# Sixteen zeroing DMAs moved to another stage, and the first use of gathered expert rows moved by eight tiles

## What is computed

```python
def peer_ffn(x, wq, subkeys, u_tab, v_tab):
    q = (xf @ wq).astype(f32).reshape(n, PEER_HEADS, 2, PEER_HALF)
    s = jnp.einsum('nhpd,hpkd->nhpk', q, subkeys.astype(f32))
    top_s, top_i = lax.top_k(s, PEER_TOPK)
    ...
    expert = jnp.take_along_axis(cand_i, best_j, axis=-1)
    gate = jax.nn.softmax(best_s, axis=-1)
    ...
    def one_block(args):
        xb, eb, gb = args
        h = jax.nn.gelu(jnp.einsum('nd,nhkd->nhk', xb, u_tab[eb], preferred_element_type=f32), approximate=False)
        return jnp.einsum('nhk,nhkd->nd', (gb * h).astype(xb.dtype), v_tab[eb])
```

## Time and profile before

| | us |
|---|---|
| median of 3 runs (3161.84 to 3166.44) | 3165.94 |
| the profiled execution | 3163.14 |
| its span | 3161.5 |
| TensorE busy | 2820.4 (89%) |
| VectorE busy | 1805.1 (57%) |
| ScalarE busy | 986.4 (31%) |
| GpSimd busy | 772.3 (24%) |

### The profile page before, as it was taken

One profiled execution on the slowest core, in us unless ns is written; L12 is line 12 of the kernel. 1 busy time (PEld: TensorE's weight loads), 2 busy tenths in 40 slices (PEclk: granted clock), 3 DMA queues, 4 the chain that ended last, 5 costly groups with the idle time before them and its releaser, 6 DMA issues.

```text
span 3161.5 us, 45193 instructions
## 1 busy us (share of the span) xinstructions
PE 2820.4 (89%) x17548; PEld 2427.2 (77%) x17548; DVE 1805.1 (57%) x2598; ACT 986.4 (31%) x1169; POOL 772.3 (24%) x630
## 2 busy tenths in 40 slices
PE   3999984767988999759699997999999999999997
PEld 2999972456666666549599997999999888888886
DVE  3455541198774443233468895555656667666655
ACT  1454530011221111122323233333334434434343
POOL 0100002210000222200018787888840000000000
PEclk7999997687889999879899998999999999999999
DMA  3355434322223555242356666999888888876664
GB/s 124 134 185 182 160 142 126 95 68 63 62 67 107 162 154 155 77 145 105 124 166 173 177 180 173 295 300 289 296 309 304 327 303 306 308 275 249 246 237 176
DMA packets 245312, 594.93 MB, mean 188 GB/s; under 512 B 76345, under 2 KB 180162, under 8 KB 192658
## 3 DMA queue, kind: packets, MB, share of 16 engines
q1 hardware_dynamic: 173874, 484.95, 44.8%
q0 software_dynamic: 54592, 90.41, 10.7%
q10 hardware_dynamic: 16640, 16.78, 1.6%
HBM read 535.05 MB, written 56.97 MB: 187 GB/s over the span
## 4 chain that ended last, share of the span: by engine, by line
PE 31%; POOL 12%; issue 5%; DMA 3%; DVE 1%; ACT 0%; DVEq 0%; POOLq 0%
POOL expert_gates L2122 12%; PE px_bank L272 10%; PE px_bank L274 10%; PE px_bank L273 10%; PE px_bank L2178 1%; DMA expert_gates<-px_chosen,px_spot 1%; POOL px_fetch L2142 1%; DMA px_w<-in_peer_v 1%; DMA px_parts<-sample_parts 0%; DMA px_fetch<-in_peer_rows,px_spots_s 0%; ACT px_wh L2253 0%; DMA px_w<-in_peer_wq 0%; DVE px_rows L2514 0%; DMA px_w<-in_peer_u 0%; DVE px_fetch L2519 0%
## 5 line engine op out<-in xcount | busy, mean ns | idle before, releaser
L2327 DVE TENSOR_TENSOR px_w_r<-px_w,px_wh 128x2048 fp32r<-128x2048 f32 x256 | 585.8, 2291 | 278.9 <-ACT px_wh L2253 278.5
L2253 ACT ACTIVATE px_wh<-px_w 128x2048 fp32r<-128x2048 f32 x256 | 489.8, 1913 | 593.1 <-PE px_bank L274 242.3
L272 PE MATMUL px_bank<-px_high,px_wh 128*128 128x256 f32 x2048 | 584.5, 285 | 24.2 <-DVE px_w_r L2327 24.2
L2122 POOL DMA_INDIRECT expert_gates<-px_chosen,px_spot x256 | 499.0, 1949 | 430.3 <-DVE px_chosen L2401 322.9
L273 PE MATMUL px_bank<-px_low,px_wh 128*128 128x256 f32 x2048 | 581.4, 284 | 0.0
L274 PE MATMUL px_bank<-px_high,px_w_r 128*128 128x256 f32 x2048 | 581.4, 284 | 0.0
L272 PEld LDWEIGHTS px_bank<-px_high,px_wh 128*128 128x128 f32 x2048 | 395.2, 193 | 25.6 <-DVE px_w_r L2327 25.6
L272 PE MATMUL px_bank<-px_wh,px_gh 128*128 128x512 f32 x1024 | 398.5, 389 | 1.2 <-DVE px_gl L2333 1.2
L274 PE MATMUL px_bank<-px_wh,px_gl 128*128 128x512 f32 x1024 | 398.4, 389 | 0.0
L273 PE MATMUL px_bank<-px_w_r,px_gh 128*128 128x512 f32 x1024 | 398.4, 389 | 0.0
L273 PEld LDWEIGHTS px_bank<-px_low,px_wh 128*128 128x128 f32 x2048 | 395.2, 193 | 0.0
(11 more groups left out here) (392 smaller groups left out, 4352.1 us busy)
## 6 DMA issues: line engine op xcount, KB each, us to landing
px_w<-in_peer_u SPq DMA_DIRECT2D x128, 1024.0 KB, 5.4
px_w<-in_peer_v SPq DMA_DIRECT2D x128, 1024.0 KB, 4.9
pj_w<-in_w_in SPq DMA_DIRECT2D x49, 1024.0 KB, 4.9
expert_gates<-rh_empty ACTq DMA_DIRECT2D x16, 1024.0 KB, 6.4
at_values<-in_kv_pages POOLq DMA_DIRECT2D x128, 128.0 KB, 2.7
at_pages<-in_kv_pages SPq DMA_DIRECT2D x128, 128.0 KB, 2.2
out_w<-in_w_o SPq DMA_DIRECT2D x16, 1024.0 KB, 4.8
px_w<-in_peer_wq SPq DMA_DIRECT2D x16, 1024.0 KB, 4.9
```

The source lines that it names most:

```text
L272: pe.matmul(out, w_high, high, start=start, stop=False, skip_group_check=True)
L2122: pool.indirect_dma_start(gates_d, bass.IndirectOffsetOnAxis(ap=spot[:, t, z:z + 1], axis=0), chosen[:, 2, t, z:z + 1], None, compute_op=A ...
L2253: act.activation(w_high[u % WH][:], w[s][:], ACT.Copy).then_inc(raised, 1)
L2327: v.tensor_tensor(w_low[s][:], w[s][:], w_high[u % WH][:], ALU.subtract).then_inc(lowered, 1)
```

## The change

The sixteen zeroing DMAs go from the joint stage to the input projection: ScalarE issues one behind the emptying of chunks 0, 3, 6 to 45, from a tile `nothing` that GpSimd clears first of all; SyncE waits for them at the end of that phase. The old tile, its clearing on VectorE and ScalarE's wait for the DMAs at the end of the joint stage go. In the expert stage the first turn with a gathered tile is u = 50 instead of u = 42; all later turns of the samples follow, so four of the 32 additions move from the up half to the down half.

```diff
@@ in_projection @@
+        nothing = sb("nothing", [P, NP])
+        gates_to = gates_d.rearrange("(z p x n) o -> z p x (n o)", z=16, p=P, n=NP)
@@ sync @@
                 sp.wait_ge(stored, 48)
+                sp.wait_ge(gates_zeroed, 16 * 16)
@@ scalar @@
                     empty(c)
+                    if c % 3 == 0 and c // 3 < 16:
+                        act.wait_ge(nothing_set, 1)
+                        act.dma_start(gates_to[c // 3], nothing[:].rearrange("p (o n) -> p o n", o=1)
+                                      .to_broadcast([P, D // NP, NP])).then_inc(gates_zeroed, 16)
@@ gpsimd @@
+                pool.memset(nothing[:], 0.0).then_inc(nothing_set, 1)
@@ mixers @@
-        empty = sb("empty", [P, NP])
@@ scalar @@
                     done(act.activation(wu_out(0), wu_in(0), ACT.Copy, scale=-1.0), i, "wu")
-                    act.wait_ge(emptied, 1)
-                    for z in (2 * i, 2 * i + 1):
-                        act.dma_start(gates_to[z], empty[:].rearrange("p (o n) -> p o n", o=1)
-                                      .to_broadcast([P, D // NP, NP])).then_inc(cleared, 16)
...
-                act.wait_ge(cleared, 32 * PAIRS)
@@ vector @@
-                v.memset(empty[:], 0.0).then_inc(emptied, 1)
@@ peer_layer @@
     def sample_turn(u):

         if u < NK:
-            return u >= 42 and u % 2 == 0
+            return u >= 50 and u % 2 == 0
         return u % 3 == 1
```

More of the change, by code:

```diff
@@ L373, in build @@
                 cx.phase(split, "x_in", xT, before_mix, x_low)
-                cx.phase(in_projection, a, o, projT, ends, before_mix, x_low, ident, feat_d, post_d, rows_d)
+                cx.phase(in_projection, a, o, projT, ends, before_mix, x_low, ident, feat_d, post_d, rows_d, gates_d)
             bias_rows, vnew_d, mask_d = (scratch(*x) for x in (
@@ L383, in build @@
             cx.phase(mixers, a, o, projT, mixT, ident, ends, feat_d, post_d, rows_d,
-                     (bias_rows, vnew_d, mask_d, wrow, ws, vrows, qi, qb, near, table), gates_d)
+                     (bias_rows, vnew_d, mask_d, wrow, ws, vrows, qi, qb, near, table))
         with ExitStack() as late:
@@ L396, in build, with in_projection @@
         peer(cx, a, o, mixT[:, :, META:N], mixT, ident, gates_d)
-def in_projection(cx, a, o, projT, ends, high, low, ident, feat_d, post_d, rows_d):
+def in_projection(cx, a, o, projT, ends, high, low, ident, feat_d, post_d, rows_d, gates_d):
     nc = cx.nc
@@ L431, in in_projection @@
                  "up_done", "gated", "keyed", "exped", "producted", "normed", "rooted", "featured", "turned", "rowed",
-                 "stored_features", "stored_rows", "link", "stored")
+                 "stored_features", "stored_rows", "link", "stored", "nothing_set", "gates_zeroed")
         (constants, raised, lowered, summed, emptied, cleared, differed, mixed, squashed, up_done, gated, keyed, exped,
          producted, normed, rooted, featured, turned, rowed, stored_features, stored_rows, link,
-         stored) = (cx.sem(f"pj_{x}") for x in names)
+         stored, nothing_set, gates_zeroed) = (cx.sem(f"pj_{x}") for x in names)
         groups = [[C_WA, C_WA + 1, C_WA + 2]] + [[j, 8 + j, 16 + j] for j in range(PAIRS)]
@@ L750, with mixers @@
 HOOKS = 21
-def mixers(cx, a, o, projT, mixT, ident, ends, feat_d, post_d, rows_d, tables, gates_d):
+def mixers(cx, a, o, projT, mixT, ident, ends, feat_d, post_d, rows_d, tables):
     nc = cx.nc
@@ L803, in mixers @@
         zeroed, stored = cx.sem("rh_zeroed"), cx.sem("rh_stored")
-        emptied, cleared = cx.sem("rh_emptied"), cx.sem("rh_cleared")
-        gates_to = gates_d.rearrange("(z p x n) o -> z p x (n o)", z=2 * PAIRS, p=P, n=NP)
         def chunk_rows(c):
```

## The result

| | median us | lowest to highest | ratio to before, 95% interval |
|---|---|---|---|
| before | 3163.89 | 3159.83 to 3166.44 | |
| after | 3131.34 | 3124.93 to 3138.32 | 0.9899 [0.9874, 0.9924] |

32.6 us faster; the forecast was 23.5 us and 3142, its range 3133 to 3156, so the sign and the larger term held and the size did not. The profiled execution of after has a span of 3128.2 us, 33.3 us less than before.

The account below looks back on a forecast made before the run. It took GpSimd's scatter of gates, reaching TensorE through one gathered tile, to pace part of the expert stage. 16.9 + 3.8 + 2.8 = 23.5 us off the 3165.9 us median gave 3142 us, range 3133 to 3156.

Parts of the forecast that it names:

- Part 1: Expert stage: first gathered tile at u = 50 instead of 42 removes TensorE's waits for lowered weights, 16.9 us gained.
- four more turns in the down half: Expert stage, second half: VectorE's four extra turns of about 2.3 us cost 0, at most 9.2 us.
- turn 0: Joint stage: zeroing pair delays the last key page by 4.0 us; removing it books 3.8 us.
- part 2: Joint stage: sixteen zeroing DMAs leave; 3.8 and 2.8 us gained, at most 14.3 us.
- Turn 7: Joint stage: last value page used 3.48 instead of 6.28 us after issue without the zeroing pair, 2.8 us gained.
- Turns 1 to 6: Joint stage: no longer TensorE wait stands behind a zeroing pair there, so 0 gained.
- part 3: Input projection: the sixteen zeroing DMAs placed there cost 0; 10.2 us if ScalarE's slack were gone.
- Rival B: Joint stage gives nothing, its TensorE waits filled by SyncE's loads or VectorE instead: 3149 us; chance 0.17.
- Rival C: Joint stage gives all of its 14.3 us bound, ScalarE's hold included: 3135 us; chance 0.10.
- Rival D: Expert stage: VectorE waits as long at u = 50, and the joint stage gives nothing: 3166 us; chance 0.05.
- Rival F: Input projection: weight tiles come late beside the zeroing writes, 38 us of waits: 3180 us; chance 0.04.
- rival E: Expert stage: GpSimd falls behind at 13.6 us per turn, VectorE waits 40 us: 3182 us; chance 0.04.

Follow-up runs that it names:

- e1: The kernel before with only the first gathered tile moved to u = 50, zeroing left in the joint stage: 3142.60 us beside 3160.72, ratio 0.9946.
- e6: The kernel before, TensorE filling its waits for key units 5, 6 and 7 of turn 0 with unread matmuls: 3163.85 us beside 3165.75, ratio 0.9992.
- e2: The kernel after with the first gathered tile back at u = 42, so only the zeroing is moved: 3148.52 us, ratio 0.9968.
- e5: The kernel after, unchanged, measured again: 3132.23 us beside 3165.75 for the kernel before, ratio 0.9899.
- e14: The kernel after, unchanged, measured once more: 3138.14 us beside 3157.18 for the kernel before, ratio 0.9940.

## Why the prediction was right in its sign and too small

**Part 1 held.** 16.9 us were booked, 17.2 measured in the first pair of traces, 17.7 over eighteen, 18.1 in e1's median. VectorE's wait and the 5.76 us tiles came as described. GpSimd waits for VectorE ahead of the fourth gather, as described, but for 7.0 us and not 1, since its gathers started 5.4 us earlier, counted from the first query matmul, and once more for 9.7 us when the gathers of output vectors begin; neither reached TensorE. GpSimd's last scatter is issued at 2312.1 us, and SyncE's reload at 2397.07 does not wait for it. The four more turns in the down half cost nothing visible (730.4 us from the reload to the end before, 731.2 after).

**The step that failed is turn 0 in part 2: "I book 3.8 us".** The wait was read rightly: 6.23 became 2.32 us, and 2.8 us of it were kept at unit 7. They were kept by GpSimd's earlier start on that unit's pages; that the 3.77 us wait there goes, as the prediction has it, is not so in this trace (3.01). What it left out is what the clock does behind the waits. In part 1 I had included it, since the long tile holds it; in turn 0 I priced idle time alone, though the earlier trace rows shows two 1.92 us rows for what elsewhere takes 1.05. The term was 11.0 us in the early course, three traces against five, with 3.1 of 10.9 as the wait and 7.8 as half clock in the first pair. e6's one early trace agrees: it gives 8.8 us back with every transfer left in place. That the medians of e6 do not leaves open how often the clock takes this part. The Trainium skill, TensorE: Matmul & The Clock Gate, under "HAM oscillation — how this bites in real kernels", has the rule: a wait for a DMA between two bursts lowers the clock, and the next burst starts at the lower one. The traces agree in kind: 16.00 us of matmuls at 0.50 behind the waits of before, 57.6 instead of 66.4 us once they are filled.

**Turn 7 was a smaller miss:** 4.2 us, booked 2.8. The yardstick was turn 6's 3.48 us from issue to start. After, turn 7 has 2.44 and turn 6 still has 3.39 (1176.31 to 1179.70), with no zeroing in either. Turn 6's last page itself lands later, 3.3 us after its issue against 2.4 in turn 7, while the DMA engines are busy 0.67 of the time (1176 to 1180 us) against 0.32 (1269 to 1272) and SyncE issues `at_pages` beside it. That these loads are the reason is not tested.

**Turns 1 to 6, 0, and part 3, 0, held.** From unit 9's last matmul to the wait at turn 7 the nine traces that zero in turns 1 to 6 take 647.9 to 653.4 us (mean 650.7), the nine that do not 643.7 to 653.9 (mean 649.6): 1.0 us, well inside their spread. The projection has 0.7 us. Rival B is out, by e2 and by the turn 7 waits. Rival C had the total nearly right, 3135, for a wrong reason: its 6 x 2 x 0.64 = 7.7 us for ScalarE's hold in turns 1 to 6 are not there. Rival D is out, since VectorE's wait is gone. Rival F is out: the projection's weight tiles land after 6.2 us at the median, 4.9 before, and after 11.1 at the longest, as before, though the zeroing writes there take 6.7 to 15.6 us, more than the 11.4 that the prediction had as the worst. For rival E, GpSimd slower beside VectorE, the prediction cites the Trainium skill, SBUF — State Buffer ("Who interferes with whom"): the engine that issues second blocks. No slower pace is seen: the scatter's median is 1.571 us, 1.550 before.

**The sum, remade:** 17.7 + 11.0 + 4.2 - 0.7 = 32.2 us in the early course, which is what the first comparison and e5 measured (32.6 and 33.5), and 17.7 + 2.9 + 4.2 - 0.7 = 24.1 in the late one, nearer to e14's 19.0. If before ran early and after late, it is 17.7 + (66.8 - 69.2) + 4.2 - 0.7 = 18.8, which fits e14 too. The forecast's 23.5 lies between the comparisons, but it was made of a term that is right in neither course. And its base was narrow: three executions within 4.6 us of each other told nothing of the 35 us over which 29 executions of the same kernel spread. That the course makes the difference between whole comparisons is an inference, since each run has a trace of one of its executions only.

## What to carry to other kernels

Price a wait of TensorE together with the matmuls behind it: look at the granted clock of the stretch that follows, and at whether the same matmul takes 1.05 or 1.92 us there. Here two bulk writes beside small loads that TensorE waits for cost 11.0 us in the early course, where the delay itself was 3.9; sixteen beside dense matmuls, with slack in the issuing engine, cost 0.7. Where a stage's clock goes up and down, take a second trace of the same kernel before explaining a difference of a few microseconds by a change.

## What the runs showed of the hardware that was not expected

- The idle gap itself was the smaller part: some 3 us less waiting went with 17.1 us of half clock that fell away (599.4 to 616.5 us before, with TensorE busy 16.00 of them).
- The same program has two courses of one stage, told apart some 45 us ahead of the waits that make the difference: 4.7 or 6.3 us of the same matmuls without any idle time, then, where nothing is zeroed or filled there, 55 to 56 or 69 to 70 us for one later stretch. What decides between them is open.
- Twice sixteen 1 MB writes beside the projection's weight loads cost 2.7 us in all (385.0 against 382.3 us).
